# A decoder trunk's feed-forward stage, 1072 columns split into four groups of 268 instead of three of 358

## What is computed

```python
def sqrelu_mlp(h, w_up, w_down):
    return jnp.square(jax.nn.relu(h @ w_up)) @ w_down
...
    for i in range(DEPTH):            # DEPTH = 2
        ...                           # token mixer, x += mixer(rms_norm(x))
        xp = xp + sqrelu_mlp(rms_norm(xp, norm_mlp[i]), mlp_w_up[i], mlp_w_down[i])
        xs = xs + sqrelu_mlp(rms_norm(xs, norm_mlp[i]), mlp_w_up[i], mlp_w_down[i])
```

## Time and profile before

| | |
|---|---|
| time, median of 3 runs | 2685.18 us (2683.98 to 2685.26) |
| span of the profiled execution | 2681.8 us |
| median less that span | 3.4 us |
| PE busy | 2570.8 us, 96% of the span, 15690 matmuls |
| PEld busy | 2465.3 us, 92%, 15690 weight loads |
| DVE busy | 1060.1 us, 40% |
| ACT busy | 565.7 us, 21% |
| DMA | 149.77 MB, mean 56 GB/s |

### The profile page before, as it was taken

The page is one execution under the profiler, slowest core; times in us unless marked ns, Lnnn a source line. Parts: engine busy times, 40 slices in busy tenths (PEclk is TensorE's granted clock), DMA queues, the critical chain, the costliest instruction groups (busy, mean ns, idle before and its releaser), DMA issues. The chain is left out here.

```text
span 2681.8 us, 35958 instructions
## 1 busy us (share of the span) xinstructions
PE 2570.8 (96%) x15690; PEld 2465.3 (92%) x15690; DVE 1060.1 (40%) x1234; ACT 565.7 (21%) x930; POOL 67.6 (3%) x56
## 2 busy tenths in 40 slices
PE   6899989999999999999999999899999999999998
PEld 6896769899999999999999987679899999999998
DVE  5235842433333333335523325643433333333433
ACT  5334832211011111103300112212211111101111
POOL 0001420000000000000000000000000000000000
PEclk8997989999999999999999989979999999999999
DMA  8412002110111111111311230141111111111101
GB/s 170 140 32 82 1 4 98 48 48 31 47 47 47 39 39 47 47 47 33 112 48 32 72 123 32 40 145 48 48 33 46 47 47 47 36 42 47 47 31 65
DMA packets 119524, 149.77 MB, mean 56 GB/s; under 512 B 23625, under 2 KB 94325, under 8 KB 119156
## 3 DMA queue, kind: packets, MB, share of 16 engines
q1 hardware_dynamic: 115112, 139.40, 17.0%
q0 software_dynamic: 1488, 8.87, 0.8%
q10 hardware_dynamic: 2844, 0.34, 0.1%
HBM read 122.87 MB, written 27.76 MB: 56 GB/s over the span
## 5 line engine op out<-in xcount | busy, mean ns | idle before, releaser
L1083 DVE TENSOR_TENSOR x<-x,ps 128x1074 f32<-128x1074 f32 x128 | 163.0, 1274 | 485.3 <-PE ps L296 485.1
L290 PE MATMUL ps<-act_hi,w_hi 128*128 128x358 f32 x1536 | 337.0, 328 | 16.5 <-DVE act_lo L1076 16.5
L290 PE MATMUL ps<-h_hi,w_hi 128*128 128x358 f32 x1536 | 338.4, 329 | 0.0
L290 PE MATMUL ps<-act_hi,w_lo 128*128 128x358 f32 x1536 | 335.9, 327 | 0.0
L290 PE MATMUL ps<-h_hi,w_lo 128*128 128x358 f32 x1536 | 335.9, 327 | 0.0
L248 ACT ACTIVATE w_hi<-raw 128x1024 fp32r<-128x1024 f32 x180 | 187.3, 1049 | 679.8 <-PE ps L296 507.2
L276 PE MATMUL ps<-h_hi,w_hi 128*128 128x358 f32 x864 | 296.2, 343 | 11.9 <-DVE w_lo L253 10.5
L290 PEld LDWEIGHTS ps<-act_hi,w_hi 128*128 128x128 f32 x1536 | 265.2, 189 | 21.3 <-DVE act_lo L1076 21.3
L277 PE MATMUL ps<-h_lo,w_hi 128*128 128x358 f32 x864 | 284.2, 329 | 0.0
L296 PE MATMUL ps<-act_lo,w_hi 128*128 128x358 f32 x1536 | 271.6, 325 | 0.0
L290 PEld LDWEIGHTS ps<-h_hi,w_hi 128*128 128x128 f32 x1536 | 266.5, 190 | 1.1 <-issue 1.1
(11 more groups left out here) (298 smaller groups left out, 2625.6 us busy)
## 6 DMA issues: line engine op xcount, KB each, us to landing
raw<-in_mlp_w_up SPq DMA_DIRECT2D x32, 1024.0 KB, 5.5
raw<-in_mlp_w_down SPq DMA_DIRECT2D x32, 1024.0 KB, 5.0
raw<-in_mlstm_w_in SPq DMA_DIRECT2D x12, 1024.0 KB, 5.1
x<-scratch_x SPq DMA_DIRECT2D x16, 537.0 KB, 7.0
scratch_x<-x SPq DMA_DIRECT2D x1, 4296.0 KB, 45.1
scratch_x<-x POOLq DMA_DIRECT2D x1, 4296.0 KB, 13.8
scratch_og<-stage POOLq DMA_DIRECT2D x8, 537.0 KB, 3.0
x_tok<-in_x_prompt SPq DMA_DIRECT2D x8, 512.0 KB, 8.6
```

The costliest lines, as they stand in the source:

```text
L290: nc.tensor.matmul(ps[:, bank + g, 0:TG], w_block(w, slot, k, kc, cols), hi[:, k, g * TG:g * TG + TG], start=start and i == 0, stop=False)
L1083: nc.vector.tensor_tensor(grp(x[:, o, :]), grp(x[:, o, :]), ps[:, out_banks(n):out_banks(n) + 3, 0:TG], ALU.add).then_inc(out_free, 1)
```

## The change

In the feed-forward loop alone, the 1072 columns are taken in four groups of `TQ = 268` instead of three of 358. The two padding columns are no longer computed there. One output block fills four banks, blocks with even `o` banks 0 to 3, with odd `o` banks 4 to 7 (`mlp_banks`). Since these overlap banks that the neighbours use, three waits come in: `out_free` up to `n0` at `o = 0` (all blocks of the projection before are emptied), `norm_ln` at `o = 1` (ScalarE has read the norm's banks 6 and 7), and `out_free` in `gates_pe` at `k == 4` ahead of the norm's matmuls. The instructions of VectorE and ScalarE read and write 1072 columns in place of 1074, and the two that read PSUM go over 4 x 268 in place of 3 x 358. Everything else stays.

```diff
+TQ = T // 4
...
+        def quarters(ap):
+
+            return ap[:, 0:T].rearrange("p (g n) -> p g n", g=4)
...
+        def mlp_banks(o):
+            return 4 * (o % 2)
...
             for i, w in enumerate((w_hi, w_lo)):
-                for g in range(3):
-                    nc.tensor.matmul(ps[:, bank + g, 0:TG], w_block(w, slot, k, kc, cols),
-                                     hi[:, k, g * TG:g * TG + TG], start=start and i == 0, stop=False)
+                for g in range(4):
+                    nc.tensor.matmul(ps[:, bank + g, 0:TQ], w_block(w, slot, k, kc, cols),
+                                     hi[:, k, g * TQ:g * TQ + TQ], start=start and i == 0, stop=False)
 
         def pass_lo(slot, k, kc, cols, bank, lo, stop):
 
-            for g in range(3):
-                last = nc.tensor.matmul(ps[:, bank + g, 0:TG], w_block(w_hi, slot, k, kc, cols),
-                                        lo[:, k, g * TG:g * TG + TG], start=False, stop=stop)
+            for g in range(4):
+                last = nc.tensor.matmul(ps[:, bank + g, 0:TQ], w_block(w_hi, slot, k, kc, cols),
+                                        lo[:, k, g * TQ:g * TQ + TQ], start=False, stop=stop)
             return last
...
-                    nc.scalar.activation(act_hi[:, j, :], relu[j % 2][:, :], ACT.Square).then_inc(up_done, 1)
+                    nc.scalar.activation(act_hi[:, j, 0:T], relu[j % 2][:, 0:T], ACT.Square).then_inc(up_done, 1)
...
-                    nc.vector.scalar_tensor_tensor(out=grp(relu[j % 2][:, :]),
-                                                   in0=ps[:, out_banks(n):out_banks(n) + 3, 0:TG], scalar=0.0,
-                                                   in1=rstd[:, :, :], op0=ALU.max, op1=ALU.mult
+                    nc.vector.scalar_tensor_tensor(out=quarters(relu[j % 2][:, :]),
+                                                   in0=ps[:, mlp_banks(j):mlp_banks(j) + 4, 0:TQ], scalar=0.0,
+                                                   in1=quarters(rstd[:, :, :].rearrange("p g n -> p (g n)")), op0=ALU.max, op1=ALU.mult
...
-                        nc.vector.tensor_tensor(grp(x[:, o, :]), grp(x[:, o, :]),
-                                                ps[:, out_banks(n):out_banks(n) + 3, 0:TG], ALU.add
+                        nc.vector.tensor_tensor(quarters(x[:, o, :]), quarters(x[:, o, :]),
+                                                ps[:, mlp_banks(o):mlp_banks(o) + 4, 0:TQ], ALU.add
...
                     pe.wait_ge(out_free, i * 12 + (n0 + o - 1))
+                    if o == 0:
+                        pe.wait_ge(out_free, n0)
+                    if o == 1:
+                        pe.wait_ge(norm_ln, 6 * layer + 6)
...
+                if k == 4:
+                    pe.wait_ge(out_free, n)
                 if k in (4, 5, 6):
                     norm_pe(pe, 2, k - 4)
```

More of the change, by code:

```diff
@@ L1071, in mlp_slice_dve @@
                         dve.wait_ge(act_split, i * 4 + (ups + j))
-                    nc.vector.tensor_tensor(relu_sq[:, :], relu[j % 2][:, :], relu[j % 2][:, :], ALU.mult
+                    nc.vector.tensor_tensor(relu_sq[:, 0:T], relu[j % 2][:, 0:T], relu[j % 2][:, 0:T], ALU.mult
                                             ).then_inc(sq_done, 1)
@@ L1075, in mlp_slice_dve @@
                     dve.wait_ge(up_done, i * 4 + (ups + j + 1))
-                    nc.vector.tensor_tensor(act_lo[:, j, :], relu_sq[:, :], act_hi[:, j, :].bitcast(F32),
+                    nc.vector.tensor_tensor(act_lo[:, j, 0:T], relu_sq[:, 0:T], act_hi[:, j, 0:T].bitcast(F32),
                                             ALU.subtract).then_inc(act_split, 1)
@@ L1107, in mlp_slice_pe @@
                             pe.wait_ge(act_split, i * 4 + (ups + k + 1))
-                        pass_hi(slot, k, deep, slice(P * c, P * c + P), out_banks(n0 + o), hi, k == 0)
+                        pass_hi(slot, k, deep, slice(P * c, P * c + P), mlp_banks(o), hi, k == 0)
                     for k in range(deep):
@@ L1111, in mlp_slice_pe @@
                             pe.wait_ge(norm_lo, KC * (2 * layer + 1) + k + 1)
-                        last = pass_lo(slot, k, deep, slice(P * c, P * c + P), out_banks(n0 + o), lo, k == deep - 1)
+                        last = pass_lo(slot, k, deep, slice(P * c, P * c + P), mlp_banks(o), lo, k == deep - 1)
                     last.then_inc(out_ready, 1)
```

## The result

| | before | after |
|---|---|---|
| median | 2685.15 us (4 runs, 2683.98 to 2685.26) | 2743.48 us (4 runs, 2741.22 to 2745.88) |
| ratio | | 1.0222, 95% interval 1.0210 to 1.0235 |
| span of the profiled execution | 2681.8 us | 2743.9 us |

The change makes the kernel 58 us slower. The forecast was 43. It shows that the 43 were made up wrongly: the finer cut costs about half of them, and something that wasn't in the sum costs twice what the cut does.

The account below looks back on a forecast made before the run. TensorE's queue was taken as the limit in the feed-forward loops. Dearer matmuls (+2.77 us a slice) less a shorter stall (0.09) made +2.68, over sixteen slices +42.9 us, to 2728 us; range 2680 to 2745.

Parts of the forecast that it names:

- the case held likeliest: Feed-forward loops: a fixed part of 12 to 18 ns in each matmul, giving 2715 to 2745 us; chance 0.60.
- the case that gives most of the remainder to the columns: Feed-forward matmuls: the 15.1 ns beyond clock time go with columns, up to 6 ns fixed; 2680 to 2700 us, chance 0.22.
- The fixed cost of a matmul: Feed-forward loops: each matmul pays 15.1 ns whatever its width, so 268 columns take 126.8 ns; +2.77 us a slice.
- rival A: Feed-forward matmuls: the 15.1 ns belong to the columns, 123.0 ns each, no change, 2681 us; chance 0.22 with up to 6 ns fixed.
- The stall at block 4: TensorE's wait for the last hidden block's act_lo in each slice: 0.09 us shorter, 1.30 to 1.21 us.
- The added waits at 0: The new waits at o = 0, o = 1 and the gates' k = 4 are already met when TensorE arrives: 0 us.
- the sign that the prediction gave for a misread cover: TensorE waiting at o = 0 or o = 1 for more than a microsecond would show the added waits' covers were misread.
- VectorE over four pieces at 0: VectorE reading PSUM in a fourth piece costs zero; at most 60 ns in relu, 1 us over 16 slices.
- Rival B: Feed-forward loops: the weight load is no longer hidden, spacing about 135 ns, +144 us, 2829 us; chance 0.12.
- PEclk at 1.00 in both loops: Sign to check in the changed kernel's profile: TensorE's clock should stay at 1.00 in both feed-forward loops.

## Why the prediction was right or wrong

The direction was right, and the time lies in the range of 2680 to 2745 us, 1.5 us below its end. The number was 15 us too low by the medians, and 19 by the profiled spans: one term was 22 us too large, and another of 41 us was missing. That the time fell into the range, and into the 2715 to 2745 us of the case held likeliest, was luck. Moved by 40 instructions, the same cut takes 2702.5 us, which is below that case and at the upper end of the 2680 to 2700 us of the case that gives most of the remainder to the columns.

- **The fixed cost of a matmul**, the step on which all hung. The choice between "by matmul" and "by column" was posed too sharply. Measured is 125.3 ns, between 123.0 (rival A) and 126.8 (forecast), and by the line through the widths some 6 of the 13.6 ns are fixed, where the forecast had all of it fixed and its likeliest case 12 to 18 ns. Over 768 matmuls that is 1.15 us a slice less than forecast, 18 us in sixteen. The plain cost of the cut is what the shift by 40 shows: +0.73%, 19 us (15 to 24) in place of 42.9. By slices: 97.15 and 97.4 us against 95.92 and 96.05, 1.2 and 1.35 us more each, 21 us in all. The rule of the Trainium skill, "TensorE: Matmul & The Clock Gate", section "Back-to-back issue gap", N / 2.4 + 2.5 ns for an isolated stream, gives 114.2 ns at 268 columns and 215.8 at 512; the trace disagrees with both, 125.3 and 233.7.
- **Code loading**, the missing term. "No instruction changes its place" was true of the order and said nothing of how many there are. The prediction had the count of matmuls in a slice and took no look at the instruction queue, though its row stood on the page. In seven returns of layer 0's loop it costs: block 4 of the first and of the last slice lie 720.8 us apart in the changed kernel (562.85 to 1283.68) and 679.8 in the one moved by 40 (560.20 to 1240.00), so 41.0 us, 5.9 a return. Of the one at 610 us, 2.9 us are idle time; the rest is matmuls at half the clock, which falls behind the stop (mean 0.69 over 11.1 us). The medians give the same 41 us (2743.5 against 2702.5).
- **The stall at block 4.** Forecast 0.9 to 1.0 us idle, and 0.09 us shorter; measured 0.99 in place of 1.03 to 1.04, start to start 1.28 us at a spacing of 0.125 where it was 1.36 at 0.164, so 0.04 us shorter. Right in kind.
- **The added waits at 0.** Right: 1.0002 by themselves. The forecast that none would show in the profile was wrong in form, since the profile named VectorE's L1091 at just that place; so the sign that the prediction gave for a misread cover, a wait of over a microsecond at `o = 0`, came up with the covers intact. Only the run with the waits alone tells that name from a cause.
- **VectorE over four pieces at 0.** Right: `relu` 1275 ns and the down blocks' add 1272, against 1277 and 1274.

```profile
L1091 DVE TENSOR_TENSOR x<-x,ps 128x1072 f32<-128x1072 f32 x128 | 162.8, 1272 | 498.1 <-PE ps L304 498.1
...
L1073 DVE SCALAR_TENSOR_TENSOR relu<-ps,rstd 128x1072 f32<-128x1072 f32 x64 | 81.6, 1275 | 515.6 <-PE ps L304 515.6
```

- **Rival B, the load out of hiding.** It didn't come at 268 columns, and at 134 it did, at 111.7 ns, close to the transposes' 108.5.
- **Rival A's price.** It took over the stall of 1.21 us, which belongs to the forecast's 126.8 ns. At 123.0 ns the 24 matmuls that fill the time last 2.95 us as before, so that the stall stays at 1.30 us and rival A comes to about 2683 us in place of 2681; nothing else hangs on it.
- **PEclk at 1.00 in both loops.** Wrong in layer 0 (0.98 over the loop), as a consequence of the stops.

## What to carry to other kernels

Where TensorE is the limit and each matmul brings its own weight load, take as few matmuls as the banks allow and cut them evenly: here one more per 1072 columns costs about 7 ns for each run over the columns (21 us over 3072 of them), 0.7% of the kernel. Evenly, because a narrow rest pays for its load: 512, 512 and 48 columns would by the table take 2 x 233.7 + 111.7 = 579 ns, an estimate that no run here tried, against 493 for three times 358. Before a change that makes a hardware loop's body longer, count its instructions and look at the instruction queue's row: as long as the loop stays resident there are hardly any packets while it runs, and nine in a slice mean that it reloads itself. A wait at the first instruction of a loop's body that the profile lays to an engine long done, or to "issue", once for each return, is best tested by moving the code by some tens of instructions, with a move by a whole piece as the control.

## What the hardware showed beyond that

- TensorE's code comes in pieces of 16 KB, 256 instructions. A loop of 1564 instructions reloads nothing when it touches seven pieces and nine pieces a turn when it touches eight; shifts by 8, 40 and 256 instructions gave 2745, 2703 and 2742 us.
- Short stops have a price beyond themselves: from the end of the stop of 2.08 us on, the one of 0.80 us included, the granted clock was 0.50 for 6.8 us (610.3 to 617.1), and 268 columns took 223 ns instead of 125.
- A stream of 134-column matmuls with 128-column loads lost the full clock at a stop of 1.98 us and didn't get it back in the loop, though it then stood still for only 0.15 us in a slice; with 268 columns it came back each time. The loads were the floor, 111.7 ns at the full clock and 213 at half.
